# RWKV triangular inverses: 64x64 blocks in two quarters of the array, or 32x32 blocks in four with a small join

## The chip, the cores and the metric

One NeuronCore of a Trainium2 chip runs the kernel alone. Its engines are PE (TensorE; PEld is its weight load), DVE (VectorE), ACT (ScalarE), POOL (GpSimd) and SP (SyncE, which issues DMAs). Each runs its own instructions in the order in which they were written and waits on semaphores that others raise. The metric is the device time of one execution in microseconds (us). PE's clock is granted at one of two levels, 2.4 GHz (1.00) or 1.2 GHz (0.50).

## The reference

One layer step of a hybrid network on 1024 prompt tokens and 8 samples of 16 tokens: norms and projections, three mixers (a gated linear recurrence, windowed attention, RWKV), their merge, cross attention and a convolutional feed-forward. The change concerns the RWKV mixer alone, whose core is

```python
def step(S, inp):
    r_t, w_t, k_t, v_t, a_t, b_t = inp
    Sa = jnp.einsum('bhvk,bhk->bhv', S, a_t)
    S = S * w_t[:, :, None, :] + Sa[..., None] * b_t[:, :, None, :] + v_t[..., None] * k_t[:, :, None, :]
    return S, jnp.einsum('bhvk,bhk->bhv', S, r_t)
```

for 8 heads of width 64. The kernel computes it by chunks of 64 tokens (16 for a sample): within a chunk the dependence of every token on those before it is a strictly lower triangular matrix L per head, and the solution needs the inverse T of (1 - L), in fp32.

## The kernel before, in words

The program runs six stages one after the other with a barrier between them: input projection, linear recurrence, RWKV (`stage_rwkv`), merge, queries and cross attention, tail. `stage_rwkv` works on nine tiles of 128 tokens: tiles 0 to 7 are the prompt, two chunks c of 64 tokens each, tile 8 holds the samples. A round r does four things for four tiles at once: the preparation of tile r+1 (decay, low-rank products "lora", normalised keys, turned copies), the inverse of tile r, the serial part of tile r-1 (state of the recurrence, `from_state`, `solve`, `to_state`, `outputs`, once per chunk) and the group norm of tile r-2. The order on every engine is written out by hand in the loop over the rounds (L1213, L1345, L1618), so an instruction that waits holds up all that stand behind it on its engine.

The inverse of a tile: `grams` (L1473) makes the Gram products, from which ACT copies the transposed L of 16 blocks (8 heads by 2 chunks) into LT (`copy_lt`, L1183). A block is 64x64 and lies on partitions 64c to 64c+63; one matmul per block reads and writes the same 64 partitions, so that the two chunks use the two quarters on the diagonal of PE's 128x128 array. All 16 blocks together fill one tensor of 128 x 512. The inverse is built by doubling: DVE masks the 2x2 blocks out of LT (`masked_b`, L1318), PE turns them (`first_turn`, L1485), DVE adds the identity to both (`first_level`, L1334), which gives T and its transpose TT for blocks of 2. Then for n = 4, 8, 16, 32, 64: POOL masks the off-diagonal part of the n-blocks out of LT into O (`off_blocks`, L1127), PE multiplies O and T (`off_times_t`, L1493), ACT copies the product Y out of PSUM (`copy_y`, L1194), PE multiplies Y with TT for T and for TT (`merge`, L1504), DVE adds both (`merge`, L1309). The last level makes TT alone, which `solve` and the next round need. Tile 8 stops at n = 16. Each such product is 16 matmuls of 64x64 (records on PE come in pairs, two for an fp32 matmul); names read out<-moving,stationary, so `rwkv_bank<-rwkv_T,rwkv_O` is an off-block product and `rwkv_bank<-rwkv_Y,rwkv_TT` and `rwkv_bank<-rwkv_TT,rwkv_Y` are the two of a merge. All matmuls of the stage but the turns (L1470) carry line L1450.

Between the steps of the inverse the loop on PE puts the other tiles' work: `from_state` and `solve` behind the Gram products, `lora_wa` before the first merge, `to_state` and `lora_g` around the second off-block product, and so on.

## Time and profile before

| what | value |
| --- | --- |
| median of 3 runs (lowest to highest) | 2932.54 us (2931.17 to 2935.34) |
| the profiled execution | 2929.11 us |
| its span, first to last instruction | 2927.6 us |
| busy in the span: PE, DVE, ACT, POOL | 2648.8, 1336.1, 741.1, 229.4 us |
| mean granted clock of PE | 0.938 |

The profile is of one execution. Times in it run from the start of its span. A timeline row gives a group's start, the time from the start of its first instruction to the end of its last, and in brackets how long the engine stood idle before it and for whom. Groups on one engine overlap a little, since the next instruction starts before the last one's result is out; what a group costs the next is read from start to start. Busy time of PE is a modelled end of pipelined matmuls and is no measure of how well the array is used.

### The profile page before, as it was taken

What the parts mean: (1) busy time and instruction counts of PE and PEld (TensorE: products, weight loads), DVE (VectorE), ACT (ScalarE), POOL (GpSimd) and SP (SyncE); (2) the same over time, 40 slices, a digit from 0 to 9 for tenths busy, and PEclk for the clock granted to TensorE, in tenths of its full rate; (3) what the DMA queues carried; (4) which work ended last, traced back from release to release, by engine and by line L of the source; (5) the groups of instructions that cost most, each with busy time, mean ns of one, the idle gap of its engine ahead of it and who ended that gap; (6) DMA issues with size and microseconds to landing.
All of it is one profiled execution on the core that took longest, in us unless ns stands there. A gap on an engine that the chain in (4) does not pass through costs nothing. (4 is left out here: it accounts for less than half of the span.)

```text
span 2927.6 us, 49375 instructions
## 1 busy us (share of the span) xinstructions
PE 2648.8 (90%) x20480; PEld 2526.4 (86%) x20480; DVE 1336.1 (46%) x2036; ACT 741.1 (25%) x1138; POOL 229.4 (8%) x380
## 2 busy tenths in 40 slices
PE   6999999999658888759997898979999999999996
PEld 4999999999447777659997687879999999999995
DVE  5112344420756777335614503324666555654246
ACT  4111122221534444133303421122211111112122
POOL 0001110000212333100000001000000000000000
PEclk8999999999659999779998899779999999999998
DMA  3222233321630110054504125341111111123133
GB/s 126 92 85 83 91 110 107 108 95 71 131 111 28 35 35 7 12 174 149 175 22 144 74 83 203 103 147 36 44 44 67 67 67 58 54 106 113 59 97 124
DMA packets 136977, 258.87 MB, mean 88 GB/s; under 512 B 41376, under 2 KB 85200, under 8 KB 134016
## 3 DMA queue, kind: packets, MB, share of 16 engines
q1 hardware_dynamic: 103248, 185.30, 19.1%
q0 software_dynamic: 9168, 37.75, 3.8%
q10 hardware_dynamic: 24432, 33.95, 3.1%
q8 instruction: 99, 1.62, 0.2%
q14 instruction: 30, 0.25, 0.0%
HBM read 190.36 MB, written 67.52 MB: 88 GB/s over the span
## 5 line engine op out<-in xcount | busy, mean ns | idle before, releaser
L252 PE MATMUL tail_bank<-tail_x_hi,tail_w_hi 128*128 128x384 f32 x1494 | 359.6, 339 | 8.2 <-DVE tail_w_lo L179 8.2
L252 PE MATMUL tail_bank<-tail_x_hi,tail_w_lo 128*128 128x384 f32 x1494 | 358.3, 339 | 0.0
L252 PE MATMUL tail_bank<-tail_x_lo,tail_w_hi 128*128 128x384 f32 x1494 | 358.2, 339 | 0.0
L252 PE MATMUL inproj_bank<-inproj_xh,inproj_win_hi 128*128 128x384 f32 x1224 | 283.0, 340 | 0.0
L252 PEld LDWEIGHTS tail_bank<-tail_x_hi,tail_w_hi 128*128 128x128 f32 x1494 | 270.7, 188 | 11.8 <-DVE tail_w_lo L179 11.3
L252 PE MATMUL inproj_bank<-inproj_xl,inproj_win_hi 128*128 128x384 f32 x1224 | 278.6, 336 | 0.0
L252 PE MATMUL inproj_bank<-inproj_xh,inproj_win_lo 128*128 128x384 f32 x1224 | 278.5, 336 | 0.0
L252 PEld LDWEIGHTS tail_bank<-tail_x_hi,tail_w_lo 128*128 128x128 f32 x1494 | 270.9, 189 | 0.0
L252 PEld LDWEIGHTS tail_bank<-tail_x_lo,tail_w_hi 128*128 128x128 f32 x1494 | 270.7, 188 | 0.0
L252 PEld LDWEIGHTS inproj_bank<-inproj_xh,inproj_win_hi 128*128 128x128 f32 x1224 | 216.2, 189 | 2.7 <-issue 2.7
L252 PEld LDWEIGHTS inproj_bank<-inproj_xh,inproj_win_lo 128*128 128x128 f32 x1224 | 218.2, 188 | 0.0
L252 PEld LDWEIGHTS inproj_bank<-inproj_xl,inproj_win_hi 128*128 128x128 f32 x1224 | 218.2, 188 | 0.0
L174 ACT CAST tail_w_hi<-tail_w_raw 128x1024 fp32r<-128x1024 f32 (+2 forms) x100 | 92.6, 926 | 474.6 <-PE tail_bank L252 348.9
L179 DVE TENSOR_TENSOR inproj_win_lo<-inproj_win_raw,inproj_win_hi 128x1024 fp32r<-128x1024 f32 x52 | 63.5, 1223 | 250.3 <-ACT inproj_win_hi L174 250.3
L252 PE MATMUL merge_bank<-merge_operands,merge_w_hi 128*128 128x384 f32 x672 | 143.2, 340 | 12.8 <-DVE merge_w_lo L179 12.8
L179 DVE TENSOR_TENSOR tail_w_lo<-tail_w_raw,tail_w_hi 128x1024 fp32r<-128x1024 f32 (+2 forms) x100 | 106.9, 1069 | 84.4 <-ACT tail_w_hi L174 84.3
L2403 DVE TENSOR_TENSOR tail_room<-tail_bank,tail_rs 128x384 f32<-128x384 f32 x132 | 59.6, 507 | 181.8 <-PE tail_bank L252 181.5
L252 PEld LDWEIGHTS merge_bank<-merge_operands,merge_w_hi 128*128 128x128 f32 x672 | 121.4, 192 | 13.4 <-DVE xt L1853 8.4
L1740 DVE TENSOR_TENSOR xt<-tail_bank,xt 128x384 f32<-128x384 f32 x96 | 47.9, 551 | 168.5 <-PE tail_bank L252 156.0
L687 ACT COPY inproj_z<-inproj_bank 128x384 f32<-128x384 f32 x114 | 47.6, 496 | 201.9 <-PE inproj_bank L252 201.2
L252 PE MATMUL merge_bank<-merge_operands,merge_w_lo 128*128 128x384 f32 x420 | 97.1, 339 | 0.0
L252 PEld LDWEIGHTS merge_bank<-merge_operands,merge_w_lo 128*128 128x128 f32 x420 | 76.5, 192 | 0.0
(377 smaller groups left out, 4252.4 us busy)
## 6 DMA issues: line engine op xcount, KB each, us to landing
inproj_win_raw<-in_w_in SPq DMA_DIRECT2D x52, 512.0 KB, 3.3
tail_w_raw<-in_w_up SPq DMA_DIRECT2D x44, 512.0 KB, 4.3
scratch_z<-inproj_z ACTq DMA_DIRECT2D x38, 576.0 KB, 2.8
merge_gate<-scratch_z POOLq DMA_DIRECT2D x24, 576.0 KB, 4.0
scratch_h<-tail_room SPq DMA_DIRECT2D x18, 576.0 KB, 3.1
tail_room<-scratch_h POOLq DMA_DIRECT2D x18, 576.0 KB, 4.1
tail_w_raw<-in_w_down SPq DMA_DIRECT2D x24, 384.0 KB, 3.0
xq_w_raw<-in_w_mem_kv SPq DMA_DIRECT2D x16, 512.0 KB, 3.2
```

What stands on the lines that cost most here:

```text
L174: act.copy(self.hi[s][:, 0:self.kt], self.raw[s][:, 0:self.kt]).then_inc(self.rounded, 1)
L179: dve.tensor_tensor(self.lo[s][:, 0:self.kt], self.raw[s][:, 0:self.kt], self.hi[s][:, 0:self.kt].bitcast(F32), ALU.subtract).then_inc(sel ...
L252: mm = pe.matmul(self.bank[s][c][:, 0:self.tc], w[s][:, k, :], x[:, k, c * self.tc:(c + 1) * self.tc], start=(k == 0 and n == 0), stop=last)
L687: act.copy(out[s][:, c * TC:(c + 1) * TC], prod.bank[s][c][:, 0:TC]).then_inc(prod.used, 1)
L1740: dve.tensor_tensor(row, prod.bank[s][c][:, 0:TC], row, ALU.add).then_inc(prod.used, 1)
L2403: dve.tensor_tensor(u[s][:, 2 + c * TC:2 + c * TC + n], up.bank[s][c][:, 0:n], rs[:, c * TC:c * TC + n], ALU.mult).then_inc(S(f"u{s}"), 1)
```

## The change

The inverse is built in 32x32 blocks, four per 128 partitions (two chunks c by two halves h), on the four quarters of 32 on the diagonal of the array: one product is 32 matmuls of 32x32, and the tensors Ld, O, Th, ThT and Y are 128 x 256. The levels are n = 4, 8, 16, 32. Level 64 becomes a join of two halves with one off-diagonal block: its off-block product is 16 matmuls of 32x32 (`off_times_half`), and `merge_halves` makes the block of TT above the diagonal (16 matmuls) and, with an identity, moves the second half beside it (16 more), for the prompt's tiles. ACT copies the second half of L twice, once with a factor per partition that keeps the rows of the second half (Lm), once whole (Lx); DVE puts the diagonal blocks of both halves together (Ld). The 2x2 mask and the identity are applied on DVE before the turn, so that `first_level` is a plain copy. ACT assembles the 64-wide TT from both parts (`assemble`) at the end of the round, behind the copy of B's tokens; the next tile's Gram products wait for that instead of for DVE's last add, and so does the samples' part. The masks table has other columns. Row tables, sizes of buffers and counts of semaphores are left out here:

```diff
...
+        halves = [P, 2, KM, HB]
+        Ld, Lx, Lm, Th, ThT, Y = (st.sb(n, halves) for n in ("L_diag", "L_off", "L_second", "T_half", "TT_half", "Y"))
+        O_ = two("O", halves)
+        turned0 = two("from_state0", t4)
...
+        quad = lambda c, h: slice(CH * c + HB * h, CH * c + HB * h + HB)
+        quads = [(c, h) for c in range(2) for h in range(2)]
+        block32 = lambda i, p, s: slice((KM * s + p) * HB, (KM * s + p + 1) * HB)
+        HW = NH * HB
+        halfbank = lambda i: banks[i][:, 0:HW]
...
-            return [n for n in (4, 8, 16, 32, 64) if n <= (CH if t < LAST else NS)] if is_tile(t) else []
+            return [n for n in (4, 8, 16, 32) if n <= (CH if t < LAST else NS)] if is_tile(t) else []
+        whole = lambda t: 0 <= t < LAST
...
                 def off_blocks(t, i):
-                    pool.wait_ge(S("LT"), 2 * t + 2)
...
-                    tt(eight(O_[i % 2][:]), eight(LT[:]), cb(f"off{levels(t)[i]}T", NH), ALU.mult).then_inc(S("O"), 1)
+                    pool.wait_ge(S("L_diag"), 2 * t + 2)
...
+                    tt(eight(O_[i % 2][:]), eight(Ld[:]), hb(f"off{levels(t)[i]}T"), ALU.mult).then_inc(S("O"), 1)
...
                 def copy_lt(t):
                     act.wait_ge(S("grams"), 2 * t + 2)
                     if t:
-                        act.wait_ge(S("O"), merges[t])
+                        act.wait_ge(S("L_diag"), 2 * t)
                     for s in range(2):
-                        act.copy(LT[:, s], gram(5 + s, 0)).then_inc(S("LT"), 1)
+                        second = gram(5 + s, 0)[:, :, HB:CH]
+                        act.activation(Lm[:, s], second, ACT.Identity, scale=env["half_rows"][1]).then_inc(S("LT"), 1)
+                        act.copy(Lx[:, s], second).then_inc(S("LT"), 1)
+
+                def assemble(t):
+
+                    q, n = t % 2, merged(t + 1)
+                    act.wait_ge(S("T"), written(t + 1))
+                    act.activation(eight(TiT[q][:])[:, :, 0:HB], eight(ThT[:]), ACT.Identity, scale=env["half_rows"][0]).then_inc(S("TT"), 1)
+                    act.wait_ge(S("merged"), n)
+                    if whole(t):
+                        act.copy(eight(TiT[q][:])[:, :, HB:CH], halfbank(4).rearrange("p (n t) -> p n t", n=NH)).then_inc(S("TT"), 1)
+                    else:
+                        act.activation(eight(TiT[q][:])[:, :, HB:CH], eight(ThT[:]), ACT.Identity, scale=env["half_rows"][1]).then_inc(S("TT"), 1)
...
-                    act.copy(flat8(Y[:]), banks[2][:]).then_inc(S("Y_copied"), 1)
+                    act.copy(flat8(Y[:]), halfbank(2)).then_inc(S("Y_copied"), 1)
...
                     if prep:
                         copy_tokens(u, 2, Bt)
+                    if nl:
+                        assemble(t)
...
-                    dve.wait_ge(S("LT"), 2 * t + 2)
+                    dve.wait_ge(S("LT"), 4 * t + 4)
...
-                        tt(TiT[q][:, s], gram(5 + s, 0), cb("off2T", KM), ALU.mult).then_inc(S("masked"), 1)
+                        stt(out=Ld[:, s], in0=gram(5 + s, 0)[:, :, 0:HB], scalar=env["half_rows"][0], in1=Lm[:, s],
+                            op0=ALU.mult, op1=ALU.add).then_inc(S("L_diag"), 1)
+                    dve.wait_ge(S("L_diag"), 2 * t + 2)
+                    link(tt(eight(ThT[:]), eight(Ld[:]), hb("off2T"), ALU.mult))
+                    tt(eight(ThT[:]), eight(ThT[:]), hb("ident32"), ALU.add).then_inc(S("T"), 1)
...
                     dve.wait_ge(S("first_turned"), t + 1)
-                    tt(eight(Ti[:]), banks[4][:].rearrange("p (n t) -> p n t", n=NH), cb("ident64", NH), ALU.add).then_inc(S("T"), 1)
-                    tt(eight(TiT[t % 2][:]), eight(TiT[t % 2][:]), cb("ident64", NH), ALU.add).then_inc(S("T"), 1)
+                    dve.tensor_copy(flat8(Th[:]), halfbank(4)).then_inc(S("T"), 1)
...
-                    if nl > 4:
-                        merge(t, 4)
...
+                def blocks_product(bank, left, right, done):
+                    for p, s, hs in heads:
+                        for c, h in quads:
+                            r = quad(c, h)
+                            mm = mm_(banks[bank][r, block32(bank, p, s)], left[r, s, p, :], right[r, s, p, :], start=True, stop=True)
+                    mm.then_inc(done, 1)
...
+                def off_times_half(t):
+                    pe.wait_ge(S("T"), written(t + 1) - 1)
                     for p, s, hs in heads:
                         for c in range(2):
...
+                            mm = mm_(banks[2][quad(c, 1), block32(2, p, s)], Lx[quad(c, 0), s, p, :], Th[quad(c, 0), s, p, :], start=True, stop=True)
+                    mm.then_inc(S("Y"), 1)
+
+                def merge_halves(t):
+                    pe.wait_ge(S("Y_copied"), merges[t + 1])
+                    pe.wait_ge(S("T"), written(t + 1))
                     for p, s, hs in heads:
                         for c in range(2):
...
+                            r = quad(c, 1)
+                            mm_(banks[4][quad(c, 0), block32(4, p, s)], Y[r, s, p, :], ThT[r, s, p, :], start=True, stop=True)
+                            mm = mm_(banks[4][r, block32(4, p, s)], hm("ident32")[r, :], ThT[r, s, p, :], start=True, stop=True)
                     mm.then_inc(S("merged"), 1)
...
-                            pe.wait_ge(S("T"), written(t))
+                            pe.wait_ge(S("TT"), 2 * t)
                         grams(t)
...
-                    if nl > 4:
-                        off_times_t(t, 4)
+                    if whole(t):
+                        off_times_half(t)
                     if serial:
                         outputs(b)
-                    if nl > 4:
-                        merge(t, 4)
+                    if whole(t):
+                        merge_halves(t)
```

PE, the second inverse tile, from the state's product to the first merge, before (first fence) and now (second). `masks,rwkv_TT` and `masks,rwkv_TT_half` are the first turn, `rwkv_X` is `solve`, `tanh_w_and_a` is `lora_wa`.

```order
L1450 MATMUL rwkv_bank<-rwkv_V_tok,rwkv_LakT 64x64 x8
L1450 MATMUL rwkv_bank<-rwkv_state,rwkv_AR 64x64 x16
L1450 MATMUL rwkv_bank<-masks,rwkv_TT 64x64 x16
L1450 MATMUL rwkv_bank<-rwkv_X,rwkv_TT 64x64 x8
L1450 MATMUL rwkv_bank<-rwkv_T,rwkv_O 64x64 x16
L1450 MATMUL rwkv_bank<-rwkv_tanh_w_and_a,rwkv_w2a 128x128 x8
L1450 MATMUL rwkv_bank<-rwkv_Y,rwkv_TT 64x64 x16
L1450 MATMUL rwkv_bank<-rwkv_TT,rwkv_Y 64x64 x16
```

```order
L1485 MATMUL rwkv_bank<-rwkv_V_tok,rwkv_LakT 64x64 x8
L1485 MATMUL rwkv_bank<-rwkv_state,rwkv_AR 64x64 x16
L1485 MATMUL rwkv_bank<-masks,rwkv_TT_half 32x32 x32
L1485 MATMUL rwkv_bank<-rwkv_X,rwkv_TT 64x64 x8
L1485 MATMUL rwkv_bank<-rwkv_T_half,rwkv_O 32x32 x32
L1485 MATMUL rwkv_bank<-rwkv_tanh_w_and_a,rwkv_w2a 128x128 x8
L1485 MATMUL rwkv_bank<-rwkv_Y,rwkv_TT_half 32x32 x32
L1485 MATMUL rwkv_bank<-rwkv_TT_half,rwkv_Y 32x32 x32
```

The order stays; each product of the inverse has 32 matmuls of 32x32 in the place of 16 of 64x64, and `solve` between them stays at 64x64.

DVE, the same tile, behind the copy of X: the masks up to the first add of the low-rank product (`sw`), before and now.

```order
L1300 COPY rwkv_X<-rwkv_bank 64x256 x2
L1323 TENSOR_TENSOR rwkv_TT<-rwkv_bank,masks 128x256 x2
L1325 TENSOR_TENSOR rwkv_MrbT<-rwkv_bank,masks 128x256 x2
L1336 TENSOR_TENSOR rwkv_T<-rwkv_bank,masks 128x512
L1337 TENSOR_TENSOR rwkv_TT<-rwkv_TT,masks 128x512
L1342 TENSOR_TENSOR rwkv_sw<-rwkv_bank,vec 128x512
```

```order
L1331 COPY rwkv_X<-rwkv_bank 64x256 x2
L1357 SCALAR_TENSOR_TENSOR rwkv_L_diag<-rwkv_bank,masks,rwkv_L_second 128x128 x2
L1360 TENSOR_TENSOR rwkv_TT_half<-rwkv_L_diag,masks 128x256
L1361 TENSOR_TENSOR rwkv_TT_half<-rwkv_TT_half,masks 128x256
L1363 TENSOR_TENSOR rwkv_MrbT<-rwkv_bank,masks 128x256 x2
L1374 COPY rwkv_T_half<-rwkv_bank 128x256
L1379 TENSOR_TENSOR rwkv_sw<-rwkv_bank,vec 128x512
```

Two masks of 128x256 in front of the turn became two operations of 128x128 and two of 128x256, one after the other; behind the turn one copy of 128x256 stands where two operations of 128x512 stood.

ACT, the end of that round and the start of the next, before and now; `TT<-TT_half` and `TT<-bank` are `assemble`.

```order
L1203 COPY rwkv_K_tok<-rwkv_bank 128x512
L1196 COPY rwkv_Y<-rwkv_bank 128x512
L1203 COPY rwkv_B_tok<-rwkv_bank 128x512
L1284 COPY rwkv_o_tok<-rwkv_bank 128x4x64 x2
L1179 ACTIVATE rwkv_tanh_w_and_a<-rwkv_z 64x128
L1180 COPY rwkv_tanh_w_and_a<-rwkv_z 64x128
```

```order
L1225 COPY rwkv_Y<-rwkv_bank 128x256
L1232 COPY rwkv_K_tok<-rwkv_bank 128x512
L1225 COPY rwkv_Y<-rwkv_bank 128x256
L1232 COPY rwkv_B_tok<-rwkv_bank 128x512
L1212 ACTIVATE rwkv_TT<-rwkv_TT_half,masks 128x8x32
L1215 COPY rwkv_TT<-rwkv_bank 128x8x32
L1315 COPY rwkv_o_tok<-rwkv_bank 128x4x64 x2
```

Behind the copy of B's tokens stand two more operations ahead of the copies of the outputs, and the copies of Y are half as wide.

## Rows read from the trace of the kernel before

**Rows 1.** The profile's page: its span and its table of engines.

```profile
span 2927.6 us, 49375 instructions
...
PE 2648.8 (90%) x20480; PEld 2526.4 (86%) x20480; DVE 1336.1 (46%) x2036; ACT 741.1 (25%) x1138; POOL 229.4 (8%) x380
```

**Rows 2.** Busy time by stretch of the RWKV stage: us, each engine's busy us, granted clock, DMA.

```profile
855.09:891.88 36.79, 28.55 (x585) 24.44 (x585) 23.78 (x34) 14.22 (x25) 9.68 (x9) 0.84 0.11 32
...
891.88:1164.22 272.34, 242.21 (x5932) 216.23 (x5933) 200.85 (x310) 125.57 (x231) 81.82 (x71) 0.99 0.09 25
...
969.26:1009.46 40.20, 35.95 (x849) 32.22 (x849) 29.43 (x45) 18.34 (x35) 12.63 (x11) 0.96 0.11 32
...
1009.46:1048.14 38.68, 34.44 (x848) 30.75 (x849) 29.42 (x45) 18.32 (x35) 12.62 (x11) 1.00 0.12 33
...
1164.22:1189.69 25.47, 22.57 (x617) 21.06 (x617) 13.13 (x26) 7.64 (x16) 8.81 (x7) 1.00 0.05 14
...
976.46:979.87 3.41, 3.41 (x50) 3.29 (x49) 2.21 (x2) 1.17 (x2) 2.51 (x2) 0.50 0.28 82
```

**Rows 3.** Timeline of PE in one round: start, us, group, idle before and its releaser.

```profile
1009.46 1.10 PE L1450 MATMUL rwkv_bank<-rwkv_AR,rwkv_K 64*64 64x128 f32 x32 [0.72 <-ACT rwkv_B_tok L1203]
...
1010.35 1.08 PE L1450 MATMUL rwkv_bank<-rwkv_AR,rwkv_B 64*64 64x128 f32 x32
...
1014.76 1.15 PE L1450 MATMUL rwkv_bank<-masks,rwkv_TT 64*64 64x64 f32 x32 [1.51 <-DVE rwkv_TT L1323]
...
1015.74 1.09 PE L1450 MATMUL rwkv_bank<-rwkv_X,rwkv_TT 64*64 64x64 f32 x16
...
1016.70 1.15 PE L1450 MATMUL rwkv_bank<-rwkv_T,rwkv_O 64*64 64x64 f32 x32
...
1017.78 1.16 PE L1450 MATMUL rwkv_bank<-rwkv_tanh_w_and_a,rwkv_w2a 64*128 64x128 f32 x16
...
1018.87 1.15 PE L1450 MATMUL rwkv_bank<-rwkv_Y,rwkv_TT 64*64 64x64 f32 x32
...
1019.86 1.10 PE L1450 MATMUL rwkv_bank<-rwkv_TT,rwkv_Y 64*64 64x64 f32 x32
...
1035.91 1.15 PE L1450 MATMUL rwkv_bank<-rwkv_T,rwkv_O 64*64 64x64 f32 x32 [0.79 <-DVE rwkv_T L1314]
...
1038.92 1.15 PE L1450 MATMUL rwkv_bank<-rwkv_Y,rwkv_TT 64*64 64x64 f32 x32 [1.16 <-ACT rwkv_Y L1196]
```

**Rows 4.** Timeline of PE's weight loads (PEld) where one product follows another.

```profile
1003.72 0.43 PEld L1450 LDWEIGHTS rwkv_bank<-rwkv_U,rwkv_B_tok 64*64 64x64 f32 x12
...
1004.02 0.13 PEld L1450 LDWEIGHTS rwkv_bank<-rwkv_T,rwkv_O 64*64 64x64 f32 x1
```

**Rows 5.** Timeline of DVE in the same round.

```profile
1013.97 0.73 DVE L1323 TENSOR_TENSOR rwkv_TT<-rwkv_bank,masks 128x256 f32<-128x256 f32 x2
...
1016.57 1.69 DVE L1337 TENSOR_TENSOR rwkv_TT<-rwkv_TT,masks 128x512 f32<-128x512 f32 x1
...
1021.00 0.69 DVE L1316 TENSOR_TENSOR rwkv_TT<-rwkv_bank,rwkv_TT 128x512 f32<-128x512 f32 x1 [0.24 <-PE rwkv_bank L1450]
...
1026.74 0.69 DVE L1316 TENSOR_TENSOR rwkv_TT<-rwkv_bank,rwkv_TT 128x512 f32<-128x512 f32 x1 [0.24 <-PE rwkv_bank L1450]
...
1031.05 3.35 DVE L1415 RECIPROCAL rwkv_sq<-rwkv_sq 128x512 f32<-128x512 f32 x1
...
1035.16 0.69 DVE L1314 TENSOR_TENSOR rwkv_T<-rwkv_bank,rwkv_T 128x512 f32<-128x512 f32 x1
```

**Rows 6.** Timeline of POOL in the same round.

```profile
1016.44 1.26 POOL L1131 TENSOR_TENSOR rwkv_O<-rwkv_LT,masks 128x512 f32<-128x512 f32 x1
```

**Rows 7.** Timeline of ACT in the same round.

```profile
1011.94 0.63 ACT L1188 COPY rwkv_LT<-rwkv_bank 128x256 f32<-128x256 f32 x2
...
1047.46 0.59 ACT L1203 COPY rwkv_B_tok<-rwkv_bank 128x512 f32<-128x512 f32 x1 [2.80 <-PE rwkv_bank L1470]
```

**Rows 8.** Timeline of PE just after the granted clock fell, one round earlier.

```profile
976.51 1.97 PE L1450 MATMUL rwkv_bank<-rwkv_T,rwkv_O 64*64 64x64 f32 x32
```

More of the change, by code:

```diff
@@ L74, in shape_masks @@
     blocks = [m[n].astype(np.float32) for n in MASKS]
-    blocks += [np.concatenate([m[n][:CH, :CH], m[n][CH:, CH:]]).astype(np.float32) for n in BLOCK_MASKS]
+    for names, size in ((BLOCK_MASKS, CH), (HALF_MASKS, HB)):
+        blocks += [np.concatenate([m[n][i:i + size, i:i + size] for i in range(0, P, size)]).astype(np.float32) for n in names]
+    halves = ((t // HB) % 2 == np.arange(2)[None, :]).astype(np.float32)
     col = np.arange(KM * P)[None, :] + np.zeros((P, 1), int)
@@ L1073, in levels @@
         def levels(t):
-            return [n for n in (4, 8, 16, 32, 64) if n <= (CH if t < LAST else NS)] if is_tile(t) else []
-        merges = [sum(len(levels(u)) for u in range(t)) for t in range(TT + 1)]
-        merged = lambda t: sum(2 * len(levels(u)) - 1 for u in range(t))
-        written = lambda t: sum(2 * len(levels(u)) + 1 for u in range(t))
+            return [n for n in (4, 8, 16, 32) if n <= (CH if t < LAST else NS)] if is_tile(t) else []
+        whole = lambda t: 0 <= t < LAST
+        masks_before = [sum(len(levels(u)) for u in range(t)) for t in range(TT + 1)]
+        merges = [sum(len(levels(u)) + whole(u) for u in range(t)) for t in range(TT + 1)]
+        merged = lambda t: sum(2 * len(levels(u)) + (1 if whole(u) else -1) for u in range(t))
+        written = lambda t: sum(2 * len(levels(u)) + 2 - (not whole(u)) for u in range(t))
         with nc.Block() as block:
@@ new lines, in off_times_t, with merge @@
+                def off_times_t(t, i):
+                    pe.wait_ge(S("T"), written(t) + (2 if i == 0 else 1 + 2 * i))
+                    pe.wait_ge(S("O"), masks_before[t] + i + 1)
+                    if i == 0:
+                        pe.wait_ge(S("masked"), 6 * t + 6)
+                    blocks_product(2, O_[i % 2], Th, S("Y"))
+                def merge(t, i):
+                    pe.wait_ge(S("Y_copied"), merges[t] + i + 1)
+                    pe.wait_ge(S("T"), written(t) + 2 + 2 * i)
+                    if whole(t) or i < len(levels(t)) - 1:
+                        blocks_product(2, ThT, Y, S("merged"))
+                    blocks_product(4, Y, ThT, S("merged"))
@@ L2521, in hybrid_stream_step @@
                "resets": [masks[:, MR + i * KM * P:MR + (i + 1) * KM * P] for i in range(2)],
-               "sample_rows": masks[:, MR + 2 * KM * P:MW]}
+               "half_mask": lambda n: masks[:, MH + HALF_MASKS.index(n) * HB:MH + (HALF_MASKS.index(n) + 1) * HB],
+               "sample_rows": masks[:, MR + 2 * KM * P:MW - 2],
+               "half_rows": [masks[:, MW - 2 + h:MW - 1 + h] for h in range(2)]}
         for stage in (stage_in_projection, stage_lru, stage_rwkv):
```

79 lines of the change are left out of this document (32 added, 47 removed).

## The prediction

> **What bounds the kernel now.** I read the page first: a span of 2927.6 us with PE busy 90% of it [rows 1]. The change alters work in the RWKV stage alone, whose inverses run from 855 to 1190 us. Then the busy times by round, from one tile's Gram products to the next: the seven rounds with all work in them last 272.3 us together, one of them 40.2 and the other six 38.7, in which PE is busy 34.4, DVE 29.4 and ACT 18.3 [rows 2]. So PE leads, but it waits over 4 us a round, and DVE is close behind. The reader is to see in [rows 3] where PE waits in the round that starts at 1009.46: 1.51 us for DVE's first mask, 0.79 for DVE's T of the third merge, 1.16 for ACT's copy of Y, and 0.72 for ACT's copy of B before the next round's Gram products. All else on PE is back to back. The inverse's fifteen products (first turn, five off-block products, nine merge products) take 0.96 to 1.08 us each from start to start, some 15 us of the 38.7.
>
> The profiled execution took 2929.11 us, 3.4 under the median of 2932.54; the sum is made against it and carried over to the median. A difference of 0.2%, 5.9 us, is what counts as faster or slower.
>
> **The price of a product in quarters.** One matmul is two records. Sixteen records that all use one 64x64 quarter (X,TT) take 15.74 to 16.70, 60 ns each; the 32 records of T,O or Y,TT use two quarters and take hardly longer (0.99 to 1.08), so a quarter still turns out a record per 60 ns or so. The Gram products use all four quarters with 128 columns: 32 records in 0.89 us, 111 ns per record on each quarter [rows 3]. So quarters run side by side, and the time of a record on its quarter follows its columns: 60 ns for 64, 111 for 128. Halving once more, I take 32 ns for a 32-column record with 32 columns of weights. A new product has 32 matmuls, 64 records, 16 on each of four quarters: 16 x 32 ns = 0.51, with the start 0.54 us, against 1.00 now. That is the low end.
>
> The other end is the rate at which records can be handed out at all. No row shows 8 ns per record. The Gram rows show 28 ns, which the quarters explain; the nearest row is [rows 4]: the first weight load of U,B_tok starts at 1003.72 and that of the next product, on an idle quarter, at 1004.02. If the stream is handed out in order, the 16 records between passed in 0.30 us, 19 ns each, and were then still held back by two busy quarters. Ends: 0.54 us, and 64 x 28 ns = 1.78. I take 0.54, since every rate seen is explained by quarters that were full and the spacing in [rows 4] is already under the Gram rate. The Trainium skill's page "TensorE: Matmul & The Clock Gate" (Part 1, "Wait — 56ns, not 53.3ns?") speaks against this: matmuls never start closer than about 25 ns, however few their columns. By that a product would take 1.6 us and the change would lose; this trace's 19 ns across quarters does not agree with it, and no run here shows more.
>
> **The other edits.** Adds and copies of Y and T halve to 256 columns: DVE 0.69 (L1316) to 0.4 (half of L1323's pair, 0.73, and the overlap), ACT 0.59 (as L1203) to 0.35 (half of L1188's pair, 0.63) [rows 5, 7]. The masks on POOL halve from 1.26 [rows 6]; they were early and stay so, worth nothing except that they block DVE (below). ACT copies L in four pieces instead of two, about 0.5 us more, still done before DVE needs it at 4.5 us into the round. Added: DVE's two-step mask with an identity add, and ACT's assembly of T at the end of the tile, two operations of 256 elements, 0.35 each by the same row. The smaller table of masks is loaded long before and hidden.
>
> **Along one round**, in us from the Gram products (1009.46), before and now:
> 1. First turn 5.3, now 6.3. Before, two masks (the pair from 1013.97), and PE starts [rows 3, 5]. Now two 128x128 operations (0.4), a mask of 256 (0.4) that waits for them, and an add of 256 (0.4) that waits for the mask; and POOL's mask starts at the same moment. L1337 took 1.69 where its size asks 0.69, beside POOL's L1131 [rows 5, 6]: POOL's ends at 1017.70 and DVE's at 1018.26, so a DVE operation from SBUF to SBUF seems to stand until POOL's is over. Ends: 0.6 later without that collision, 1.3 with all of POOL's halved 0.65; I take 1.0. Solve is queued behind the turn on PE.
> 2. The first merge's adds end at 12.2, now 11.5: four products save 1.8 on PE, and the adds and the copy of Y some 0.5; the lora products and solve (1.1 and 1.0) stay, and each change from 64- or 128-row work to quarters of 32 costs some 0.09 (T,O to lora 1.08 against 0.99 within one kind), five of these here: 1.0 - 1.8 - 0.5 + 0.5 leaves 0.8, of which I count 0.7.
> 3. The second merge's adds end at 18.0, now 16.3: three products save 1.4 of PE time, of which 1.0 reaches here, since DVE's scan and kh chain now comes last.
> 4. The third merge's first add at 25.7 [rows 5], now 23.85. Here DVE's reciprocal (3.35 us, L1415) with its copy of X before and the product after it is on the path, not PE; the faster products of this level gain nothing, and PE's wait of 0.79 grows to some 1.7.
> 5. The fourth merge on PE at 29.5 [rows 3], now 26.85: one product and shorter adds and copies, 0.8 more.
> 6. The next Gram products at 38.7, now 35.0. The merge (two products, 0.9) and the halves' level save some 1.9: the off-block product of 16 small matmuls on two quarters 0.55 instead of 1.03, the join of 32 matmuls 0.55 to 0.6 instead of 1.03. Against it stand the assembly, 0.7 behind ACT's copy of B (0.59, [rows 7]), because the Gram products now wait for it too, and a change of kind, 0.1: 1.1 more.
>
> So 3.7 us a round. **The clock takes part of it back.** One round lasted 40.2 instead of 38.7: the granted clock stood at 0.50 (1.2 of 2.4 GHz) from 976.46 to 979.87, right after that round's 1.5 us wait for the mask, and T,O took 1.97 us instead of 1.15 [rows 2, 8]. One fall costs 1.5 us. PE's wait there grows to 2.5 us, and the waits of steps 4 and 5 (1.7, then 0.4 and 1.1, with a short product between) become a second such place. I take 0.9 falls a round, 1.4 us; ends none and three. Net 2.3 us x 7 rounds (891.88 to 1164.22) = 16. The first inverse round (36.8 us, no serial work, partly at half clock) and the last tile (25.5 us, three levels) [rows 2] gain some 2 us each: 20 in all. 2929.1 - 20 = 2909, or 2912 at the median.
>
> **Rivals.**
> (a) Slower: PE hands out records no faster than the Gram products show, whatever quarter they go to. A product is then 64 x 28 ns = 1.78 us, thirteen of them add 10 us a round and the halves' level 0.65, while the waits stay as they are: some 11 x 7 and 12 in the two other rounds, 3020. At the 19 ns of [rows 4] a product is 1.2 us, a round 3.5 us longer and the time 2960. The turning point is near 14 ns per record, 0.9 us a product: the 2 us that PE then saves go into the later first turn, the assembly and the changes of kind. For it: nothing faster is seen. Against it: every slow rate has its full quarters as a reason. Chance 0.15. By the rule of 25 ns from the Trainium skill's page named above it would be this case, between the two times.
> (b) The clock falls more than twice a round, since PE has more and longer waits. At 2.5 falls nothing is left: 2932; if each fall lasts through twice the stretch, 10 to 15 us are lost, 2945. For it: one fall in seven rounds already now, after a wait of 1.5 us. Against it: the dense stretches after each gap (Gram products, lora, merges). Chance 0.17, of which 0.10 ends within 0.2% and 0.07 above.
> (c) No falls and no collision on POOL's side: 3.7 to 4.3 us a round and some 3 for the two others, 36 less: 2896. Chance 0.12.
> (d) The gain is hidden: DVE's chain of steps 3 and 4 takes more than I think (its linked operations, its waits for ACT's table loads) and the assembly delays each round by more than 0.7. Price: 2 us a round more, a net of about 0 to 4 us, 2930. Chance 0.06.
>
> **The numbers.** My own forecast, 2897 to 2926, has 0.50. Faster by over 0.2%: 0.50 + 0.12 from (c) + 0.02 from (d) = 0.64; within 0.2%: 0.10 from (b) + 0.04 from (d) = 0.14; slower: 0.15 + 0.07 = 0.22. The likeliest is 2912. The range from 2893 to 2950 leaves out the best of (c) and (a) beyond its mild part. The likeliest case's own range is 2897 to 2926.
>
> **What would show it.** A product of 64 records of 32x32 that takes 0.5 to 0.6 us from start to start shows the price right; over 0.85, (a). Rounds near 36.4 us on the mean, 35.0 where the clock is full throughout; the first turn 6.0 to 6.6 after the Gram products; PE waiting at the third merge for DVE and at the round's start for ACT's assembly (and no longer for B's copy alone); DVE's L1374 a plain copy of 0.4. The granted clock of the stage's rounds tells (b): 0.96 is one fall, under 0.90 is more than two. The prediction is wrong if the rounds are not under 38 us while products are at 0.55: then DVE or ACT, not PE, set the round.

## The result and the profile of the changed kernel

The change makes the kernel slower: a median of 2996.24 us of 4 runs (2989.6 to 2997.9) against 2933.28 us of 4 runs (2931.17 to 2935.34). The ratio is 1.021, with a 95% interval of 1.0193 to 1.0228. The profiled execution took 2997.9 us; its mean granted clock is 0.912 (0.938 before). The first lines of its page answer to [rows 1]:

```profile
span 2996.4 us, 57140 instructions
...
PE 2672.6 (89%) x24352; PEld 2538.2 (85%) x24352; DVE 1305.5 (44%) x2037; ACT 741.4 (25%) x1174; POOL 201.9 (7%) x372
```

PE has 3872 more matmul records (24352 less 20480) and as many more weight loads; DVE and POOL have less to do, as meant. Busy times by stretch (columns as in [rows 2]: us, then busy us of PE, PEld, DVE, ACT and POOL, granted clock, DMA) show where the time went:

```profile
856.99:895.39 38.40, 26.21 (x1033) 21.02 (x1033) 20.26 (x34) 14.25 (x30) 6.87 (x8) 0.72 0.13 34
...
895.39:1221.96 326.57, 260.80 (x9069) 225.31 (x9069) 174.73 (x310) 125.70 (x259) 58.75 (x64) 0.80 0.08 22
...
1177.86:1221.96 44.10, 35.84 (x1297) 30.84 (x1297) 25.43 (x45) 18.57 (x40) 8.39 (x8) 0.85 0.04 10
...
1221.96:1250.05 28.09, 23.54 (x732) 21.45 (x733) 10.69 (x25) 5.06 (x13) 5.04 (x5) 0.57 0.04 13
...
1208.63:1215.45 6.82, 5.87 (x191) 4.69 (x178) 3.54 (x7) 1.45 (x3) 0.00 (x0) 0.50 0.02 5
```

The seven full rounds take 326.57 us instead of 272.34 [rows 2], 54.2 of the 68.8 us by which the span is longer; the first inverse round adds 1.6 and the last tile 2.6. A round takes 46.7 us on the mean (44.1 to 51.0) where 36.4 was forecast. Two things are new. The granted clock is 0.80 instead of 0.99: a mean of 0.80 between the levels 1.00 and 0.50 is 40% of the time, some 131 us, at half clock, and the last row is one such stretch, 6.8 us long, in the fastest round. And a full round has 1297 records on PE instead of 849. The timeline of PE in that round answers to [rows 3]:

```profile
1177.86 1.99 PE L1485 MATMUL rwkv_bank<-rwkv_AR,rwkv_K 64*64 64x128 f32 x32 [1.54 <-ACT rwkv_TT L1215]
...
1186.01 0.75 PE L1485 MATMUL rwkv_bank<-masks,rwkv_TT_half 32*32 32x32 f32 x64 [2.69 <-DVE rwkv_TT_half L1361]
...
1201.39 0.75 PE L1485 MATMUL rwkv_bank<-rwkv_T_half,rwkv_O 32*32 32x32 f32 x64
1202.07 1.12 PE L1485 MATMUL rwkv_bank<-rwkv_rk,masks 128*128 128x512 f32 x2
...
1207.35 0.33 PE L1485 MATMUL rwkv_bank<-rwkv_T_half,rwkv_O 32*32 32x32 f32 x16 [1.40 <-DVE rwkv_T_half L1345]
1208.39 0.73 PE L1485 MATMUL rwkv_bank<-rwkv_T_half,rwkv_O 32*32 32x32 f32 x48 [0.71 <-issue]
...
1211.12 1.08 PE L1485 MATMUL rwkv_bank<-rwkv_Y,rwkv_TT_half 32*32 32x32 f32 x64 [0.95 <-ACT rwkv_Y L1225]
...
1221.96 0.34 PE L1485 MATMUL rwkv_bank<-rwkv_AR,rwkv_K 64*64 64x128 f32 x4 [1.78 <-ACT rwkv_TT L1215]
```

At full clock an off-block product takes 0.68 us from its start to that of the next work (1201.39 to 1202.07, the change of kind included) instead of 1.08. So the new products are cheap, as forecast. But the product of 1207.35 stops after 16 of its 64 records for 0.71 us, released by "issue": PE waits there for nothing that the profile shows. At 1208.63, just behind this wait and the 1.40 us before it, the half-clock stretch begins. The waits of all engines over the seven rounds (total us, times, longest) have these lines of interest, first after, then before:

```profile
PEld rwkv_bank L1485 <- issue: 52.2, 69, 2.1
...
PE rwkv_bank L1485 <- DVE rwkv_TT_half L1361: 18.9, 7, 2.7
PE rwkv_bank L1485 <- issue: 18.8, 23, 2.0
...
PE rwkv_bank L1485 <- ACT rwkv_TT L1215: 12.6, 8, 1.8
```

```profile
PEld rwkv_bank L1450 <- issue: 19.2, 36, 0.9
...
PE rwkv_bank L1450 <- DVE rwkv_TT L1323: 10.6, 7, 1.5
```

Before, PE's matmuls have no such wait for issue at all, only its weight loads do. The DMA view of one round names what may lack, queue 8 (packets, MB, share); first 1177.86 to 1221.96 of the change, then the round of [rows 3] before:

```profile
q8 instruction: 10, 0.16, 1.6%
```

```profile
q8 instruction: 6, 0.10, 1.1%
```

That this queue brings PE's instructions shows in its packets over the whole program, now and before:

```profile
q8 instruction: 129, 2.11, 0.3%
```

```profile
q8 instruction: 99, 1.62, 0.2%
```

30 packets more for 3872 records and 3872 weight loads more are 258 instructions a packet; at 16 KB a packet that is some 64 bytes each.

The side engines behave as costed. On DVE the mask of 256 columns takes 0.42 us and the identity's addition 0.83, beside POOL's mask (last row), which answers to the collision of [rows 5, 6]:

```profile
1184.67 0.42 DVE L1360 TENSOR_TENSOR rwkv_TT_half<-rwkv_L_diag,masks 128x256 f32<-128x256 f32 x1
1185.12 0.83 DVE L1361 TENSOR_TENSOR rwkv_TT_half<-rwkv_TT_half,masks 128x256 f32<-128x256 f32 x1
...
1184.71 0.96 POOL L1149 TENSOR_TENSOR rwkv_O<-rwkv_L_diag,masks 128x256 f32<-128x256 f32 x1 [12.17 <-DVE rwkv_L_diag L1357]
```

### The profile page after: what moved, and what is told of

Read it like the earlier page. It is cut to its first block and busy times, and to the rows that moved or that the text cites. A ratio compares the mean times of both kernels' runs of the same rounds, so it can differ in the third digit from the quotient of the medians.

```text
span 2996.4 us, 57140 instructions
## 1 busy us (share of the span) xinstructions
PE 2672.6 (89%) x24352; PEld 2538.2 (85%) x24352; DVE 1305.5 (44%) x2037; ACT 741.4 (25%) x1174; POOL 201.9 (7%) x372
```

## The experiments

Three theories stood. **Theory 1**: the clock. PE waits longer in single pieces (2.7 us where it was 1.5), the clock falls, and what follows takes up to twice as long. **Theory 2**: the supply of instructions. A product has twice as many instructions in half the time, and PE outruns what queue 8 brings. **Theory 3**: the longer chain of DVE and ACT (masks, assembly) sets the round. Ratios below are to runs of the kernel before on the same chip in the same session (its medians there were 2930.3 to 2934.9). Rounds and clock are those of the one profiled execution, which for e1 lies 12 us under the median, for e3 8 us over it and for the others of this table within 5.

| run | ratio to before (95%) | seven rounds, us | clock there |
| --- | --- | --- | --- |
| the change | 1.0210 (1.0193 to 1.0228) | 326.6 | 0.80 |
| e1, e11: change, PE kept working | 1.0194 (1.0174 to 1.0215), 1.0133 (1.0108 to 1.0159) | 310.4, 305.9 | 0.93, 0.95 |
| e3: change, half the instructions a product | 1.0043 (1.0026 to 1.0060) | 286.4 | 0.85 |
| e5: both | 0.9944 (0.9923 to 0.9964) | 255.9 | 0.99 |
| e7, e8: T by DVE; with PE kept working | 1.0075 (1.0047 to 1.0104), 0.9964 (0.9950 to 0.9978) | 289.4, 259.0 | 0.79, 0.98 |
| e10: e8, first round too | 0.9934 (0.9913 to 0.9954) | 258.8 | 0.99 |
| e9: before, PE kept working | 0.9985 (0.9973 to 0.9998) | 271.4 | 1.00 |

### e1 and e11: the change with PE kept working in its waits

```diff
+                def warm(n, bank):
+                    for _ in range(n):
+                        mm_(banks[bank][:, HW:2 * HW], ident, env["resets"][0][:, 0:HW], start=True, stop=True)
...
+                            warm(5, 2)
                         first_turn(t)
...
+                        warm(4, 1)
                     if nl > 3:
                         off_times_t(t, 3)
...
+                        warm(2, 1)
                     if nl > 3:
                         merge(t, 3)
...
                         turn(5, lambda ct: B[:, ct, :], S("tok"))
+                    if whole(t) and t:
+                        warm(3, 2)
```

That is e11, in the full rounds; e1 has 4, 3, 2, 3, all but the last in bank 3, where the sums of `outputs` are open, and so changes these sums.

> The changed kernel, with matmuls that compute nothing wanted put into PE's long waits of each full round: 4 of 128x256 ahead of the first turn, 3 ahead of the fourth off-block product, 2 ahead of the fourth merge and 3 ahead of the next Gram products (12 a round; no operand depends on the round). Theory 1 (the granted clock is most of the loss: it falls two to four times a round because PE stands idle longer, and everything at half clock takes twice as long): the mean granted clock from 895 to 1222 us rises from 0.80 to above 0.93, a round goes from 46.7 us on the mean to 39 to 41, the time to 2940 to 2960. Theory 2 (PE is short of instructions: the products have twice as many, and PE stands still for 'issue' inside them): the clock rises little, the waits for issue stay near 70 us over the seven rounds, the rounds stay above 44 us, the time 2975 to 3000. Theory 3 (the longer chain of DVE and ACT sets the round): the clock rises, but a round stays above 43 us, since the extra matmuls only fill waits that are set elsewhere; 2965 to 2985.

> The fourth corner of the square of change, e3 and e5: the changed kernel with exactly the extra matmuls of e5 (5, 4, 2 and 3 of 128x256, in banks that nothing else uses at that time), its products left at 32 matmuls each. If a round with 1297 wanted records cannot be shorter than instructions arrive (e6: 128 records per 3.57 us, 28 ns each, so 36.3 us a round plus 1 us for the extra ones), the clock rises to 0.92 or more and yet a round stays at 42 to 45 us with PE waiting for issue 25 to 40 us over the seven rounds: 2975 to 2992, a gain of 5 to 20 us where the same matmuls gave e3 34 us. If the clock is the main loss and e1 only fell short because its extra matmuls were too few, rounds of 38 to 41 us: 2940 to 2960.

Medians: e1 2989.46 us, e11 2969.75. Two rounds of e11, its seven rounds together, and the wait of PE's matmuls for issue:

```profile
1025.65:1073.32 47.67, 41.01 (x1325) 34.92 (x1325) 25.29 (x45) 18.23 (x40) 9.19 (x10) 0.89 0.11 29
...
1158.29:1200.18 41.89, 36.92 (x1324) 31.04 (x1325) 25.10 (x45) 18.21 (x40) 7.95 (x8) 1.00 0.04 11
894.26:1200.18 305.92, 270.71 (x9264) 228.92 (x9265) 173.41 (x310) 124.82 (x259) 58.11 (x64) 0.95 0.09 23
```

```profile
PE rwkv_bank L1485 <- issue: 30.3, 31, 2.7
```

The extra matmuls do hold the clock (0.95 instead of 0.80), and the waits for DVE and ACT are filled, yet a round still takes 43.7 us, and 41.9 in the round shown at full clock (40.8 and 41.6 in two others). The matmuls' waits for issue grow from 18.8 to 30.3 us: the faster PE works, the longer it waits for instructions. The extra matmuls alone are worth 20.7 us of 54.2. Of what was expected, e1's time and rounds came out as theory 2 had them and its clock as theory 1 had it; e11's time lies between the two ranges. Theory 3 is not settled here, since the extra matmuls stand just where PE would be seen to wait for DVE and ACT; e5 settles it.

### e2: the kernel before with twice the instructions

The other two kinds of product are cut in the same way.

```diff
-                            mm = mm_(banks[4][rows(c), (KM * s + p) * CH:(KM * s + p + 1) * CH], Y[rows(c), s, p, :],
-                                     TT_[rows(c), s, p, :], start=True, stop=True)
+                            for h in range(2):
+                                at_, of = (KM * s + p) * CH + HB * h, slice(HB * h, HB * h + HB)
+                                mm = mm_(banks[4][rows(c), at_:at_ + HB], Y[rows(c), s, p, :], TT_[rows(c), s, p, of], start=True, stop=True)
```

> The kernel before, with each of its 14 off-block and merge products of a tile cut into two halves of columns: 32 matmuls (64x64 weights, 32 columns) instead of 16 of 64 columns. The results, the order and the work of DVE, ACT and POOL stay the same; only PE's number of instructions is that of the change. Theory 2: stalls for issue appear inside and behind the products as in the changed kernel (50 to 70 us over the seven rounds, against some 20 before), and the rounds go from 38.7 us to 43 to 46, the time to 2965 to 2990. Theories 1 and 3: the products stay near 1.0 us and the rounds near 38.7 to 40, the time 2930 to 2945; if the shorter records alone make a product longer (1.2 us, say), a round is 3 us longer with no stalls for issue, 2955.

Median 3136.41 us, ratio 1.0693 (1.0656 to 1.0729), far above all that was expected, and not by stalls for issue: PE's matmuls have none. The one round at full clock and its second merge product:

```profile
1100.68:1151.23 50.55, 47.15 (x1296) 43.87 (x1297) 28.79 (x45) 18.43 (x35) 12.63 (x11) 1.00 0.09 27
```

```profile
1112.91 2.05 PE L1451 MATMUL rwkv_bank<-rwkv_TT,rwkv_Y 64*64 64x32 f32 x64
```

64 records of 32 columns take 2.0 us on two quarters, 62 ns each on its quarter, as long as records of 64 columns took in the kernel before. So with 64x64 weights half the columns save nothing; a record's time does not follow its columns alone, as the prediction had it. A round has 1297 records here too, but they are spread over 50.6 us, 39 ns for each. As a test of theory 2 in the form "many instructions" the run fails: what counts is the rate. The other rounds stood partly at half clock (58 to 72 us), although PE was busy 94% of the time and its waits did not grow; the seven rounds and the longest of the waits, which was 10.6 us before too:

```profile
926.65:1353.29 426.64, 402.81 (x9069) 375.04 (x9069) 196.88 (x310) 126.30 (x231) 81.42 (x71) 0.81 0.06 17
```

```profile
PE rwkv_bank L1451 <- DVE rwkv_TT L1324: 10.6, 7, 1.5
```

So longer waits are not needed for a low clock, and theory 1 does not say all of what lowers it.

### e6: how fast instructions come

```diff
+                    for p, s, hs in 15 * heads if t == 4 else []:
+                        for c, h in quads:
+                            mm = mm_(banks[4][quad(c, h), block32(4, p, s)], ThT[quad(c, h), s, p, :], hm("ident32")[quad(c, h), :], start=True, stop=True)
```

> The changed kernel, with the first turn of one round (tile 4) made sixteen times instead of once, back to back, into the same bank: 960 more records and as many weight loads in one row, with nothing to wait for. If PE can take small matmuls at the rate seen inside one product for as long as there are some (0.51 us a product), the row lasts 8.2 us and the time grows by about 8 us, to 3004. If instructions come in packets of 16 KB no faster than one per 3.5 to 4 us once the store is used up (theory 2: in the starved rounds of the change the packets start 3.4 to 4.0 us apart), the 1920 more instructions are 7.5 packets, the row lasts 25 to 30 us with stalls for issue of 2 to 3 us about every 2 products, and the time grows by 20 to 25 us, to 3016 to 3022.

Median 3015.29 us, 19 above the change. The timeline of PE in that row:

```profile
1039.15 2.24 PE L1485 MATMUL rwkv_bank<-masks,rwkv_TT_half 32*32 32x32 f32 x243 [2.67 <-DVE rwkv_TT_half L1361]
1043.32 1.27 PE L1485 MATMUL rwkv_bank<-masks,rwkv_TT_half 32*32 32x32 f32 x128 [1.93 <-issue]
1046.77 1.93 PE L1485 MATMUL rwkv_bank<-masks,rwkv_TT_half 32*32 32x32 f32 x128 [2.18 <-issue]
1050.23 1.93 PE L1485 MATMUL rwkv_bank<-masks,rwkv_TT_half 32*32 32x32 f32 x128 [1.53 <-issue]
...
1064.63 0.42 PE L1485 MATMUL rwkv_bank<-masks,rwkv_TT_half 32*32 32x32 f32 x13 [1.53 <-issue]
```

The reader is to see the regular step. After a wait of 2.67 us PE runs through 243 records in 2.24 us, some 9 ns each with the last one's end, and then gets 128 at a time. Six rows of 128 start 3.45 to 3.75 us apart (three are left out here), 3.57 on the mean of the five steps from 1046.77 to 1064.63: 28 ns per record. 128 records and their 128 weight loads are 256 instructions, one packet of 16 KB, and queue 8 brings 8 packets in the 28 us from 1040 to 1068, one per 3.5 us:

```profile
q8 instruction: 8, 0.13, 1.8%
```

The Trainium skill says the same of the block: its page "Runtime: NRT & Kernel Launch" (Terms) has an instruction memory per engine that is refilled in 16 KiB blocks; how fast, only these rows show. The store that a wait fills is, by the 243 records, about two such blocks.

From this price I estimate the floor of a round: 1297 records x 28 ns = 36.2 us in the change. A wait of PE that outlasts the filling of the store would come on top, which no run here shows by itself; e11's rounds at full clock, 37 us by this price, took 40.8 to 41.9. Before it was 849 x 28 = 23.7 us under a round of 38.7, and invisible.

### e3 and e5: half the instructions, and both remedies

```diff
                     for p, s, hs in heads:
+                        if p % 2:
+                            continue
                         for c, h in quads:
                             r = quad(c, h)
-                            mm = mm_(banks[bank][r, block32(bank, p, s)], left[r, s, p, :], right[r, s, p, :], start=True, stop=True)
+                            out = slice((KM * s + p) * HB, (KM * s + p + 2) * HB)
+                            mm = mm_(banks[bank][r, out], left[r, s, p, :], right[r, s, p:p + 2, :], start=True, stop=True)
```

> The changed kernel, with its blocks products (not the first turn and the halves' level) made of 16 matmuls of 32x32 weights and 64 columns instead of 32 of 32 columns: two heads share the weights of the first, so that half of the heads get products that are not theirs. A quarter turns out as many columns as in the change, with half the instructions. Theory 2: the stalls for issue fall to some 25 us over the seven rounds, and with them most falls of the clock: rounds of 37 to 40 us, the time 2915 to 2945. Theory 1: the waits for DVE and ACT stay (2.7 us at the first turn, 1.4 at the third merge, 1.8 at the Gram products), so the clock still falls at least twice a round, rounds of 42 to 45 us, 2960 to 2985. Theory 3: as theory 1, with rounds above 42 us even where the clock stays up.

> Both remedies at once: the wide products of e3 (16 matmuls of 32x32 weights and 64 columns, half of the heads with products that are not theirs) and extra matmuls in PE's waits as in e1 (5 of 128x256 ahead of the first turn, 4 ahead of the fourth off-block product, 2 ahead of the fourth merge, 3 ahead of the next Gram products; now in banks that nothing else uses at that time). If the clock (theory 1) and the supply of instructions (theory 2) are all of the loss, the granted clock of the seven rounds goes from 0.85 to above 0.95 and a round from 40.9 us to 37 to 38.5, the time from 2946 to 2918 to 2930, the gain over the kernel before that was predicted, or near it. If the chain of DVE and ACT sets the round (theory 3), the clock rises and a round stays above 40 us: 2940 or more.

Medians: e3 2945.58 us, e5 2911.2. The seven rounds of e3 together, then the last round of e5 and its seven together, and the wait of PE's matmuls for issue in e5:

```profile
891.89:1178.31 286.42, 235.06 (x6380) 200.38 (x6381) 172.65 (x310) 124.97 (x259) 60.86 (x64) 0.85 0.09 24
```

```profile
1109.68:1145.22 35.54, 34.72 (x940) 28.94 (x941) 24.94 (x45) 18.13 (x40) 8.41 (x8) 1.00 0.04 11
889.32:1145.22 255.90, 246.05 (x6576) 204.66 (x6577) 171.81 (x310) 124.37 (x259) 60.90 (x64) 0.99 0.10 27
```

```profile
PE rwkv_bank L1485 <- issue: 4.0, 7, 0.9
```

Four rows of e5's last round, for the length of its products and the path:

```profile
1116.17 0.75 PE L1485 MATMUL rwkv_bank<-masks,rwkv_TT_half 32*32 32x32 f32 x64 [0.34 <-DVE rwkv_TT_half L1361]
...
1117.93 0.65 PE L1485 MATMUL rwkv_bank<-rwkv_T_half,rwkv_O 32*32 32x64 f32 x32
1118.51 1.16 PE L1485 MATMUL rwkv_bank<-rwkv_tanh_w_and_a,rwkv_w2a 64*128 64x128 f32 x16
...
1136.58 0.65 PE L1485 MATMUL rwkv_bank<-rwkv_Y,rwkv_TT_half 32*32 32x64 f32 x32
```

Halving the instructions of twelve products, 913 records a round instead of 1297, alone takes 40.2 us off the seven rounds, though the waits for DVE (18.9 us at the first turn, as in the change) and with them many of the falls of the clock stay (0.85). Not all of it is supply: a wide product takes 0.58 us (1117.93 to 1118.51) instead of 0.68, and with twelve of them a round that is some 8 us over the seven. Both remedies take 70.7 us off, more than 40.2 + 20.7, because each hides part of the other: a PE at half clock waits less for instructions (18.8 us in the change, 30.3 in e11), so with the clock up the stalls take back part of the gain, and with the stalls gone the extra matmuls hold the clock better (0.99 against 0.95). Then the rounds are at 36.6 us on the mean, 2.3 under before; with the change's own products it would be some 37.8, still under before, so theories 1 and 2 together are the whole loss. e3's time is at the upper end of what theory 2 had, with a clock nearer to theory 1; e5's is 7 us under the range given for both. Theory 3 falls: DVE and ACT do the same work here as in the change (busy 171.8 and 124.4 us against 174.7 and 125.7), and it fits into these rounds.

### e7, e8 and e10: fewer instructions with nothing left out

```diff
+                    if whole(t) or i < len(levels(t)) - 1:
+                        dve.wait_ge(S("T"), written(t) + 3 + 2 * i)
+                        dve.transpose(flat8(Th[:]), flat8(ThT[:])).then_inc(S("T"), 1)
...
-                    if whole(t) or i < len(levels(t)) - 1:
-                        blocks_product(2, ThT, Y, S("merged"))
                     blocks_product(4, Y, ThT, S("merged"))
```

The first turn goes in the same way. e8 adds `warm` (4 ahead of the first off-block product, 4, 2, 3 as in e11), e10 has it in the first inverse round too.

> The changed kernel with fewer PE instructions and the right result: T is no longer made by PE. The first turn (64 records) and the product of T in each of the four merges (64 records each) go; in their place DVE transposes T^T in blocks of 32x32 behind its addition (256 columns an operation, as many DVE operations as before). A full round has 977 matmul records instead of 1297. Theory 2: stalls for issue fall from 52 us over the seven rounds (weight loads) to some 25 to 30, as in e3, and a round from 46.7 us to 40 to 42: 2940 to 2955. Theory 1: PE stands idle longer than ever, the clock falls to 0.80 or less, and a round stays at 43 to 45: 2965 to 2980. Theory 3: the transposition follows the addition, so each level's chain is 0.4 to 0.5 us longer on DVE; that alone costs up to 2 us a round.

> e7 with extra matmuls of 128x256 in PE's waits of the full rounds (4 ahead of the first off-block product, 4 ahead of the fourth, 2 ahead of the fourth merge, 3 ahead of the next Gram products). If clock and instructions are the whole loss: clock above 0.95 in the seven rounds, 37 to 39 us a round, 2915 to 2932, about as fast as the kernel before or somewhat faster. If the longer chain on DVE decides: the clock above 0.95 and rounds of 40 us or more, 2940 and above. If the extra matmuls do not hold the clock, as e7 within 5 us.

> e8 with extra matmuls also in the first inverse round, which has no serial work and runs at 0.70 of the clock (8 ahead of the first off-block product, 4 ahead of the third, 2 ahead of the fourth, 2 ahead of the fourth merge, 3 ahead of the next Gram products). If the clock is what that round loses, it goes from 34.0 us to 31 to 32 and the next from 38.4 to 37.5 (it begins at half clock now): 2 to 4 us less than e8, 2916 to 2918. If the round is set by DVE's and ACT's chain, nothing: 2920 within 2 us.

Medians: e7 2948.35 us, e8 2919.77, e10 2913.31 (2910.97 to 2918.71, 6 runs). The seven rounds of e7 and its matmuls' wait for issue, then the seven rounds of e10 behind its first inverse round:

```profile
893.24:1182.65 289.41, 235.43 (x6828) 200.05 (x6829) 175.33 (x310) 124.67 (x259) 59.09 (x64) 0.79 0.09 24
```

```profile
PE rwkv_bank L1484 <- issue: 1.1, 2, 0.7
```

```profile
857.38:888.36 30.98, 26.97 (x750) 21.58 (x750) 20.64 (x34) 14.93 (x31) 6.90 (x8) 0.89 0.15 40
888.36:1147.14 258.78, 234.13 (x7011) 195.33 (x7011) 173.62 (x310) 123.77 (x258) 60.07 (x64) 0.99 0.10 26
```

e7 runs at the change's clock (0.79) and its rounds are 37.2 us shorter. That is not the supply alone: the matmuls' waits for issue go from 18.8 us to 1.1, and five products a round go from PE, each up to the 0.68 us measured above, at most 24 us over the seven. e8 adds the clock, 30.4 us more, as e5 did to e3 (30.5). e10 leaves nothing out and is 0.66% faster than the kernel before, 2.7% faster than the change by the two ratios; its first inverse round went from 34.0 us in e8 to 31.0.

### e9 and e4: what does not explain it

e9 puts `warm` (3, 1, 2, 1) into the same four places of the kernel before.

> The control: the kernel before, with extra matmuls of 128x256 in its own shorter waits of the seven full rounds (3 ahead of the first turn, 1 ahead of the fourth off-block product, 2 ahead of the fourth merge, 1 ahead of the next Gram products). Its rounds already run at full clock but for one fall of 1.5 us in seven rounds, so if the extra matmuls only hold the clock they are worth 0 to 2 us here: the time within 0.2% of before, 2928 to 2934, rounds 38.7. If they did something else for the time (a release of waits, fewer stalls), this kernel would gain as much as e8 gained over e7, 20 us or more. If they get in the way of wanted work, a round is 0.3 to 0.8 us longer: 2933 to 2938.

Median 2929.95 us, 0.15% under before; the one slow round, 40.2 us [rows 2], became 39.0 and the others stayed at 38.7 to 38.8. So here the extra matmuls buy the clock and next to nothing else.

e4 makes the last level of the kernel before, and it alone, a join by one block:

```diff
+                                mm = mm_(banks[2][quad(c, 1), block32(p, s)], O_[0][quad(c, 0), s, p, HB:CH], Ti[quad(c, 0), s, p, 0:HB], start=True, stop=True)
...
+                                mm = mm_(banks[4][quad(c, 0), block32(p, s)], flat8(Y[:])[quad(c, 1), block32(p, s)], TiT[t % 2][quad(c, 1), s, p, HB:CH], start=True, stop=True)
```

> The kernel before, with its last level alone changed to a join by one 32x32 block: products of 16 matmuls of 32x32 on two quarters instead of 64x64, a copy of Y of 256 columns instead of 512, and instead of DVE's addition of 512 columns two copies of 256 columns of 32 partitions each, one on DVE and one on ACT. The number of PE instructions stays that of before. All theories but one expect a gain: two products of 0.55 us instead of 1.03 and a copy shorter by 0.25, 1.0 to 1.2 us a round, 2925. If idle time on PE makes the clock fall again at the Gram products (theory 1), one fall in some rounds eats this: 2930 to 2940. Theory 2 expects no stalls beyond those of before.

Median 2932.06 us, ratio 1.0000 (0.9988 to 1.0011). Two rounds, one as most are and the first:

```profile
1048.45:1086.67 38.22, 33.97 (x848) 30.13 (x849) 29.45 (x45) 18.47 (x36) 12.63 (x11) 1.00 0.12 34
```

```profile
889.35:932.24 42.89, 38.20 (x845) 34.25 (x845) 24.72 (x40) 15.72 (x28) 9.69 (x9) 0.88 0.08 24
```

A round at full clock is 0.46 us shorter, less than half of what was expected, since each join product takes 0.62 us and the products around it pay for changes of kind; falls of the clock in three of the seven rounds, the first of which is 4.2 us longer than the 38.7 of before, ate it. The join is not what made the change slow, and does little by itself.

## Why the prediction was wrong

**The price of a product** was right in size. 0.54 us was taken, 0.63 with the 0.09 of a change of kind; 0.68 with it is measured, and rival (a), that PE hands out no more than a record per 28 ns, is wrong within a product. The reason given was too simple: the time of a record does not follow its columns alone. On its quarter a record takes 43 ns with 32x32 weights and 32 columns (0.68 us for 16), 73 with 32x32 weights and 64 columns (0.58 us for 8, e5), both with the change of kind, and 62 with 64x64 weights and 32 columns (e2); the forecast halved both at once. For the rule of 25 ns from the Trainium skill's page "TensorE: Matmul & The Clock Gate" (Part 1, "Wait — 56ns, not 53.3ns?") the trace disagrees: across four quarters some 9 ns (e6). The rows that the prediction set against it did not yet show that: in [rows 4] 16 loads were counted by the order of the program, 19 ns each, but only 12 by their starts, 25 ns each. And for more than some 240 records in a row the 28 ns of rival (a) are true (e6), for a reason that it did not have: instructions come no faster. The step that argued the two ends treated as one price what is two, one from the store and one at the rate of supply.

**The path along a round** was right where both losses are gone. In e5's last round the first turn starts 6.5 us after the Gram products (6.3 forecast), the fourth merge 26.9 (26.85 forecast), and the round takes 35.5 (35.0 forecast); before it was 38.7. Of steps 1 to 6 none failed by much, with some luck in it, since e5's products are 0.1 us shorter than the change's. DVE's collision with POOL at the first turn cost 0.4 us, about as taken. The sign named for being wrong, rounds over 38 us with cheap products, came true, but what it was to mean, that DVE or ACT set the round, did not.

**The step on the clock failed.** "0.9 falls a round, 1.4 us" became some 19 us a round at half clock (131 us over seven). The waits that step named were the right ones (2.7, 1.4, 0.95 and 1.8 us); what it took from [rows 8], one fall in seven rounds, did not carry over. Rival (b) had the mechanism, with a chance of 0.17 and a price of 10 to 15 us at most; holding the clock is worth 21 us here and 30 once instructions suffice. Whether the longer waits lower the clock or the small products, which use four 32x32 quarters of the array, no run separates: the extra matmuls fill the waits and use the whole array at once, and in e2 the clock stayed low without longer waits. That part of the cause stays open.

**The supply of instructions was not in the sum at all.** The change raises a round from 849 to 1297 records, and the prediction counted them only as work for the quarters; the slow rate at which they might be handed out, its other end, was argued away. Queue 8 stood in the profile's own DMA table, and six packets in the round of [rows 3] gave no hint of a limit; the price had to be measured. Fewer instructions are worth 40.2 us over the seven rounds before the clock is held and 50.0 after it (the change to e3, e11 to e5), some 8 of each for the shorter products, so 32 to 42, against 21 to 30 for the clock. The sign came out wrong because of these two terms together: with either remedy alone the kernel is still slower than before (1.0133, 1.0043). That e5 and e10 come out beside the forecast of 2912 confirms nothing, since they are other kernels.

In the sum of rival (c) its terms make 29 to 33 us, not 36; nothing hangs on it.

Of the 68.8 us of the span, 58.4 are in the rows above. The stage's inverses begin 1.9 us later, 3.3 are lost between the last inverse and the merge stage (whose long row of matmuls begins at 1338.3 instead of 1274.7), and 5.2 behind that, where nothing was changed; no run here looks into these, and the four executions of the change differ by 8.3.

## What to carry to other kernels

Count instructions, not only columns: where small matmuls fill the array in parallel, compare the records of a loop times 28 ns with the loop's time before cutting tiles smaller, and move what another engine can do at little cost (here DVE's transposition of 32x32 blocks) off PE. When a change shortens PE's work but not the waits between, price the fall of the clock from rows at half clock and try a filler of a few wide matmuls in the waits; on a kernel whose clock holds it buys next to nothing (e9).

## What was not expected of the hardware

- PE's instructions arrive in packets of 16 KB, 128 records with their weight loads, one per 3.57 us when PE is starved; 243 records ran without a stop after a wait of 2.67 us (e6).
- 64 records of 32x32 on four quarters take 0.68 us, the change of kind included, while 32-column records with 64x64 weights take 62 ns each on their quarter, no less than with 64 columns (e2).
- In e2 the granted clock was 0.81 over the seven rounds (0.99 before) in a kernel whose PE was busy 94% and waited no longer than before; why was not tried.
- A matmul that starts new sums in the second half of a bank seems to spoil open sums in the first half of that bank: with such matmuls in bank 3 the first output of e1 is off by a relative 0.85, and in e11, with other banks, it is right.
